# Each batch of the gate map is multiplied between the two expert chunks of its turn

## What is computed

```python
def peer_ffn(x, w_q, sub_keys, u_tab, v_tab):
    ...
    qh = (xc @ w_q).reshape(Ct, H, 2, PEER_QDIM // 2)
    s = jnp.einsum("nhad,akd->nhak", qh, sub_keys).astype(f32)
    top_s, top_i = lax.top_k(s, K)
    ...
    best_s, pos = lax.top_k(cand, K)
    eidx = jnp.take_along_axis(cand_idx, pos, axis=-1)
    gate = jax.nn.softmax(best_s, axis=-1)
    ug = u_tab[eidx]
    vg = v_tab[eidx]
    hpre = jnp.einsum("nd,nhkd->nhk", xc, ug).astype(f32)
    act = (gate * jax.nn.gelu(hpre, approximate=False)).astype(x.dtype)
    return jnp.einsum("nhk,nhkd->nd", act, vg)
```

## Time and profile before

| | us |
|---|---|
| median of 3 runs | 1833.99 |
| lowest and highest | 1830.77, 1834.78 |
| the profiled execution, its own time | 1833.53 |
| its span, first to last instruction | 1831.7 |

### The profile page before, as it was taken

The page is one execution under the profiler, slowest core; times in us unless marked ns, Lnnn a source line. Parts: engine busy times, 40 slices in busy tenths (PEclk is TensorE's granted clock), DMA queues, the critical chain, the costliest instruction groups (busy, mean ns, idle before and its releaser), DMA issues.

```text
span 1831.7 us, 37775 instructions
## 1 busy us (share of the span) xinstructions
PE 1782.5 (97%) x13634; PEld 1674.5 (91%) x13634; DVE 1377.0 (75%) x2489; ACT 874.6 (48%) x1348; POOL 19.6 (1%) x40
## 2 busy tenths in 40 slices
PE   8999999999999999999999999999999999999998
PEld 8999999988999999988899999999999888878886
DVE  5788889855888877355767699977777689985665
ACT  4343335355343374565563645454444344444544
POOL 0000000010000000000100000000000000000000
PEclk9999999999999999899999999999999999999999
DMA  5545555432555546332235345554544455455553
GB/s 201 194 153 191 172 186 170 161 104 73 188 176 179 187 159 221 105 104 70 69 128 173 123 165 172 170 185 162 168 165 171 142 170 182 167 165 188 192 194 137
DMA packets 79997, 292.31 MB, mean 160 GB/s; under 512 B 8928, under 2 KB 9088, under 8 KB 79664
## 3 DMA queue, kind: packets, MB, share of 16 engines
q1 hardware_dynamic: 79200, 287.93, 47.1%
q0 software_dynamic: 720, 3.32, 0.5%
HBM read 290.16 MB, written 1.05 MB: 159 GB/s over the span
## 4 chain that ended last, share of the span: by engine, by line
PE 81%; DVE 14%; ACT 3%; issue 1%; DMA 1%; DVEq 0%; SPq 0%; ACTq 0%
PE ps L506 19%; PE ps L455 18%; PE ps L456 17%; PE ps L457 17%; DVE m L429 5%; PE ps L1910 2%; DVE m L1813 2%; DVE m L1809 1%; PE ps L461 1%; PE ps L545 1%; DVE m L1817 1%; PE ps L1070 1%; PE ps L1069 1%; ACT m L417 1%; ACT m L603 1%
## 5 line engine op out<-in xcount | busy, mean ns | idle before, releaser
L455 PE MATMUL ps<-m,m 128*128 128x256 f32 x3312 | 958.9, 290 | 23.0 <-DVE m L429 11.2
L456 PE MATMUL ps<-m,m 128*128 128x256 f32 x3312 | 941.5, 284 | 0.0
L457 PE MATMUL ps<-m,m 128*128 128x256 f32 x3312 | 941.0, 284 | 0.0
L429 DVE TENSOR_TENSOR m<-m,m 128x1024 fp32r<-128x1024 f32 x542 | 657.1, 1222 | 257.7 <-ACT m L417 250.8
L455 PEld LDWEIGHTS ps<-m,m 128*128 128x128 f32 x3312 | 638.8, 193 | 37.9 <-issue 24.4
L417 ACT ACTIVATE m<-m 128x1024 fp32r<-128x1024 f32 x542 | 565.4, 1050 | 170.4 <-PE ps L457 155.5
L456 PEld LDWEIGHTS ps<-m,m 128*128 128x128 f32 x3312 | 638.7, 193 | 1.2 <-issue 0.2
L457 PEld LDWEIGHTS ps<-m,m 128*128 128x128 f32 x3312 | 638.1, 193 | 0.0
L506 PE MATMUL ps<-m,m 128*128 128x512 f32 x1536 | 358.8, 393 | 2.0 <-DVE m L2009 2.0
L506 PEld LDWEIGHTS ps<-m,m 128*128 128x128 f32 x1536 | 287.0, 189 | 60.6 <-issue 2.1
L1970 ACT ACTIVATE m<-m 128x256 fp32r (+1 forms) x128 | 53.4, 418 | 202.6 <-PE ps L506 194.8
(11 more groups left out here) (252 smaller groups left out, 1142.6 us busy)
## 6 DMA issues: line engine op xcount, KB each, us to landing
m<-stream SPq DMA_DIRECT2D x542, 512.0 KB, 3.3
m<-alibi_t POOLq DMA_DIRECT2D x1, 1536.0 KB, 11.4
m<-con SPq DMA_DIRECT2D x1, 1417.0 KB, 7.4
m<-xT SPq DMA_DIRECT2D x2, 512.0 KB, 8.2
y<-m SPq DMA_DIRECT2D x4, 256.0 KB, 2.6
m<-wcmpk POOLq DMA_DIRECT2D x1, 512.0 KB, 5.3
m<-wcmpv POOLq DMA_DIRECT2D x1, 512.0 KB, 5.5
m<-fin POOLq DMA_DIRECT2D x1, 512.0 KB, 4.3
```

The lines of the kernel that those rows point to most:

```text
L429: nc.vector.tensor_tensor(w_lo[:, r, :], raw[:, r, :], w_hi[:, r, :].bitcast(F32), ALU.subtract)\
L455: nc.tensor.matmul(out, lhs[0], rhs[0], start=start, stop=False, **kw)
L456: nc.tensor.matmul(out, lhs[0], rhs[1], start=False, stop=False, **kw)
L457: return nc.tensor.matmul(out, lhs[1], rhs[0], start=False, stop=stop, **kw)
```

## The change

TensorE's order in the two stages with batches. In `second`, the batch stands behind the first up chunk and ahead of the second; in `third`, behind the first down chunk and ahead of the second. What each instruction waits for stays as it is, and no other engine's program changes.

```diff
         def second(st):
-            for u in range(2):
-                expert_up_pe(pe, st, 2, HALF + u)
+            expert_up_pe(pe, st, 2, HALF)
             gates_of_batch_pe(pe, 0, st)
+            expert_up_pe(pe, st, 2, HALF + 1)
...
         def third(st):
-            for u in range(2):
-                expert_down_pe(pe, st, 2, u)
+            expert_down_pe(pe, st, 2, 0)
             gates_of_batch_pe(pe, 1, st)
+            expert_down_pe(pe, st, 2, 1)
```

## The result

| | median, us | lowest and highest | runs |
|---|---|---|---|
| before | 1832.72 | 1830.77, 1834.78 | 4 |
| after | 1846.07 | 1845.29, 1848.0 | 4 |

The changed kernel is slower: the ratio of after to before is 1.0074, 95% interval 1.0057 to 1.0092, or +13.6 us of 1832.7. The profiled execution of after took 1848.0 us with a span of 1846.2, so the two spans differ by 14.5 us; the sum had come to 14.9.

A forecast was written before the change was run, and what follows sets the result against it. TensorE, busy for 97% of the span, was taken to set the pace; 16.1 + 1.9 + 0.5 - 1.9 - 1.7 = +14.9 us on 1833.5 gave 1848.4 us (+0.8%), range 1843 to 1855.

The forecast's parts named there:

- The third stage: Third expert stage: TensorE's batch waits 0.52 us for VectorE's one-hots in 31 turns, 16.1 us (12.4 to 20.2).
- The chain of five links: Third stage, chunk end to copy, rest, one-hots, their end, TensorE's start: 0.29, 0.56, 0.34, 1.91, 0.14, sum 3.24 us against 2.72.
- The number of waits: Third stage: a stall in every turn but the first, 31 x 0.52 = 16.1 us.
- The second stage: Second stage turns: one-hots ready 0.78 us before the batch is due, so no cost per turn.
- The first batch: Start of the second stage: TensorE waits once for the first one-hots, 1.9 us; clock loss of 0 to 1.7 left out.
- Between the second and third stages: The last batch leaves the shadow of a 3.69 us wait and delays the last up chunk: +0.5 us.
- Between the third and fourth: Ahead of chunk 64: wait of 2.1 us falls to 0.2, winning 1.9, plus 1.7 of half clock: -3.6 us.
- Rival 1: TensorE swallows the stalls through slack inside a turn; only stage ends count, -1.2 us, 1832.3 us; 8%.
- Rival 2: Second stage stalls each turn too; each tenth beyond the 0.78 us cover costs 3.1 us, 0.2 gives 1854.6; 5%.
- Rival 3: Clock falls behind the short waits; one in three of 31 stalls would give 17 us, 1866 us; 7%.

The follow-up runs named there:

- the extra 0.33 us: One unused VectorE maximum over 256 elements added ahead of the third stage's one-hots: on the changed kernel 1.0143 of before, on the kernel before 1.0005.
- extra instructions: Batch moved in the second stage alone, plus a VectorE maximum ahead of that stage's one-hots: 512 elements 1.0028 of before, 1024 elements 1.0049.

## Why the prediction was right, point by point

- **The third stage.** The chain of five links was the right one, and it comes back in full each turn, as said. Measured from the copy at 1552.96: chunk end at 1552.67 by the 0.29, batch at 1555.89, 3.22 us for 3.24. In most turns it is a little shorter, so that the average wait is 0.475 and not 0.52. The link that varies is the last: from the one-hots' end to the batch it is 1554.80 + 0.97 to 1555.89, 0.12 us, in one turn and 1561.35 + 0.97 to 1562.37, 0.05, in the next. The 0.14 of the sum, read at another place, was its upper end. Two turns in six are the long ones, and two in six of the loop's batches have one more register instruction ahead of them; that the one causes the other was not tried.
- **The number of waits.** 31 were counted at the full price, but the last turn lost 0.14. On ScalarE and VectorE it is written outside the loop, and there the links are shorter: copy to rest 1657.14 to 1657.60, 0.46 for 0.56, and one-hots 1.81 for 1.91; the copy itself comes 1657.14 - 1653.62 = 3.52 us after the batch ahead of it, where it was 1650.76 - 1647.12 = 3.64 a turn earlier. The stage cost 14.4 us for 16.1.
- **The second stage.** Zero in its turns was right, its cover was 0.89 to 0.97 for 0.78. The first batch waited 1.84 us for 1.9, and kept the clock.
- **Between the second and third stages.** The 0.5 was right. What was missing is that a longer wait can also mean a longer spell at half clock: 1.1 us in the profiled pair. This term had been left at zero. The same 3 us before, then after (in the order of the earlier trace rows):

```profile
1451.00:1454.00 3.00, 3.00 (x19) 2.58 (x18) 0.00 (x0) 0.00 (x0) 0.00 (x0) 1.00 0.00 0
...
1451.00:1454.00 3.00, 3.00 (x16) 3.00 (x15) 0.00 (x0) 0.00 (x0) 0.00 (x0) 0.50 0.00 0
```

- **Between the third and fourth.** 1.9 was right, with the 0.2 us that it left ahead of chunk 64, and of the 1.7 for the clock 1.6 came.
- So the two misses, -1.7 in the third stage and +1.1 in the clock, nearly cancel: 14.9 forecast, 14.5 between the spans, 13.6 by the ratio (10.4 to 16.9 by its interval). The mechanism was right; that the sum comes within 0.4 us of the spans is luck.
- **Rival 1** (TensorE swallows the waits) falls: the 24 matmuls behind a wait take 5.71 us as before, and the extra 0.33 us showed in full. The measure that stood beside this rival is the busy share of weight loads (the Trainium skill, "Perfetto Trace Analysis", Identifying the Most-Contended Engine). Read as room in which a wait could vanish, as the prediction read it, it would have absorbed both waits; the runs disagree with that reading here.
- **Rival 2** didn't come, and its price had been wrong: in that stage only every second turn would have paid.
- **Rival 3** didn't come. Busy time and clock of the whole third stage after (in the order of the earlier trace rows): TensorE is busy but for the 9.3 us of its waits, and the clock is at 1.00.

```profile
1456.00:1660.00 204.00, 194.73 (x1256) 153.55 (x1255) 163.95 (x278) 84.82 (x124) 0.00 (x0) 1.00 0.48 157
```

## What to carry to other kernels

When an engine is asked for something earlier, follow its queue from the last thing that it has to wait for, and look whether that wait starts ahead of the new demand or behind it: here a chain of 3.2 us stood against one chunk of 2.7, on an engine with over a microsecond of idle time. Then ask where the chain is anchored: if behind the place that waits, the wait comes back in every turn, if ahead of it, the turn behind a late one is in time again. And price the two ends of a loop apart from its turns; moving a step in the last turn alone took the whole gain (-3.1 us) without the thirty waits.

## What the runs showed of the hardware

- The clock behind a wait of TensorE is not settled by the wait's length near 2 us. It fell behind 1.95 us (before) and 1.96 (second stage alone), and behind 2.27 and 2.80 (extra instructions); it stayed behind 1.94 and behind 1.68 at the first batch. The wait of the earlier trace rows stands in all twelve traces, at 1.94 or 1.95 us, in a part of the kernel that no edit touches: the clock fell behind it in two and stayed in ten. Here it is with the last turn alone moved, then with the third stage alone changed:

```profile
1108.78 0.41 PE L455 MATMUL ps<-m,m 128*128 128x256 f32 x1 [1.95 <-DVE m L429]
1109.00:1111.00 2.00, 2.00 (x11) 2.00 (x11) 2.00 (x2) 0.00 (x0) 0.00 (x0) 0.50 0.58 162
...
1108.47 0.36 PE L455 MATMUL ps<-m,m 128*128 128x256 f32 x1 [1.95 <-DVE m L429]
1109.00:1111.00 2.00, 2.00 (x19) 2.00 (x18) 2.00 (x2) 0.00 (x0) 0.00 (x0) 1.00 0.73 221
```

- Behind a wait of 3.7 us the 32 matmuls of L497 took 5.46 to 5.47 us in four traces; behind 4.2 us they took 5.24, 5.38, 6.11, 6.17, 6.60 and 6.65 in six. The half clock can hold longer there. The six differ by up to 1.4 us behind the same wait, so the 1.1 us of the profiled pair can't be laid on the longer wait alone; on average the six take 0.6 us more than the four.
- Thirty waits of 0.28 to 0.40 us, one in every 6.5 us, did not bring the clock down at all, and neither did thirty of 0.60 to 0.82 us, one in every 6.8 us, in the changed kernel with the extra instruction.
